# The norms at the entry of the second mixer: tile 0 finished ahead of tile 1's statistics, and a gate tile moved behind tile 1's transposes

## What is computed

```python
h = layer_norm(DEEPNORM_ALPHA * h + squared_relu_mlp(h, ...), ln_mlp_g[1], ln_mlp_b[1])
...
h = rms_norm(x, norm1_w[l]) * (1.0 + sc1) + sh1
...
proj = h @ w_in          # q, k, v of one branch, q, k, v and gate z of the other, more
```

## Time and profile before

| | us |
|---|---|
| median of 3 runs | 1381.76 (1381.08 to 1386.42) |
| the profiled execution's own time | 1387.08 |
| its span | 1385.3 |
| PE busy | 1334.1 (96% of the span) |
| DVE busy | 990.7 (72%) |
| ACT busy | 735.1 (53%) |

### The profile page before, as it was taken

The page is one execution under the profiler, slowest core; times in us unless marked ns, Lnnn a source line. Parts: engine busy times, 40 slices in busy tenths (PEclk is TensorE's granted clock), DMA queues, the critical chain, the costliest instruction groups (busy, mean ns, idle before and its releaser), DMA issues.

```text
span 1385.3 us, 19114 instructions
## 1 busy us (share of the span) xinstructions
PE 1334.1 (96%) x8084; PEld 1168.8 (84%) x8084; DVE 990.7 (72%) x1119; ACT 735.1 (53%) x777; POOL 131.0 (9%) x119
## 2 busy tenths in 40 slices
PE   7999999999999999999999899999999999999996
PEld 7999877799998798799998698788878888878885
DVE  6987564767878735867855745646477788888896
ACT  6655763344444546444444355734434577677673
POOL 0002543110001000100000100015200000000000
PEclk9999999999999999999999989999999999999999
DMA  8552224377877542357775254321254699999993
GB/s 331 183 185 94 95 89 158 146 285 286 310 274 294 192 152 92 122 213 273 277 252 195 103 196 149 106 93 61 66 189 157 217 353 352 335 333 346 345 364 119
DMA packets 41768, 290.29 MB, mean 210 GB/s; under 512 B 4653, under 2 KB 5061, under 8 KB 7632
## 3 DMA queue, kind: packets, MB, share of 16 engines
q1 hardware_dynamic: 35712, 252.76, 49.7%
q0 software_dynamic: 5968, 36.27, 7.0%
HBM read 286.90 MB, written 2.11 MB: 209 GB/s over the span
## 4 chain that ended last, share of the span: by engine, by line
PE 85%; DVE 9%; ACT 3%; DMA 1%; issue 1%; POOL 1%; DVEq 0%; SPq 0%; ACTq 0%; POOLq 0%
PE banks L835 24%; PE banks L837 24%; PE banks L836 24%; DVE w_lo L1617 2%; PE banks L1380 2%; PE banks L1483 1%; DMA raw<-weights 1%; ACT w_hi L392 1%; PE banks L987 1%; DVE mod L1856 1%; DVE pre_norm L1771 1%; PE banks L1163 1%; POOL tiny L2388 1%; PE banks L996 1%; PE banks L890 1%
## 5 line engine op out<-in xcount | busy, mean ns | idle before, releaser
L1617 DVE TENSOR_TENSOR w_lo<-raw,w_hi 128x2048 fp32r<-128x2048 f32 x237 | 542.3, 2295 | 120.6 <-ACT w_hi L392 119.4
L392 ACT ACTIVATE w_hi<-raw 128x2048 fp32r<-128x2048 f32 x237 | 449.9, 1909 | 24.8 <-DMA raw<-weights 24.8
L835 PE MATMUL banks<-hT_hi,w_hi 128*128 128x256 f32 x1120 | 323.8, 289 | 3.3 <-DVE w_lo L1648 3.3
L837 PE MATMUL banks<-hT_hi,w_lo 128*128 128x256 f32 x1120 | 320.0, 286 | 0.0
L836 PE MATMUL banks<-hT_lo,w_hi 128*128 128x256 f32 x1120 | 320.0, 286 | 0.0
L835 PEld LDWEIGHTS banks<-hT_hi,w_hi 128*128 128x128 f32 x1120 | 218.1, 195 | 8.2 <-issue 4.9
L836 PEld LDWEIGHTS banks<-hT_lo,w_hi 128*128 128x128 f32 x1120 | 218.1, 195 | 1.4
L837 PEld LDWEIGHTS banks<-hT_hi,w_lo 128*128 128x128 f32 x1120 | 217.7, 194 | 0.0
L835 PE MATMUL banks<-w_hi,act_hi 128*128 128x512 f32 x256 | 100.2, 391 | 0.4 <-DVE act_lo L1827 0.4
L836 PE MATMUL banks<-w_lo,act_hi 128*128 128x512 f32 x256 | 100.0, 391 | 0.0
L837 PE MATMUL banks<-w_hi,act_lo 128*128 128x512 f32 x256 | 99.7, 389 | 0.0
(11 more groups left out here) (417 smaller groups left out, 2184.2 us busy)
## 6 DMA issues: line engine op xcount, KB each, us to landing
raw<-weights SPq DMA_DIRECT2D x238, 1024.0 KB, 4.8
mod_raw<-weights POOLq DMA_DIRECT2D x24, 1024.0 KB, 5.1
ln_gain_bias<-ln_rows POOLq DMA_DIRECT2D x4, 1024.0 KB, 7.0
h<-x SPq DMA_DIRECT2D x2, 512.0 KB, 4.1
h<-x POOLq DMA_DIRECT2D x1, 1024.0 KB, 5.5
rms_gain<-rms_rows POOLq DMA_DIRECT2D x2, 512.0 KB, 6.2
h_rows<-h POOLq DMA_DIRECT2D x1, 1024.0 KB, 4.4
bias_rows<-bias_table POOLq DMA_DIRECT2D x1, 1024.0 KB, 12.4
```

What stands on the lines that cost most here:

```text
L392: A(hi[u % RING][:, :], raw[u % RING][:, :], ACT.Copy).then_inc(S["w_hi_done"], 1)
L835: mm(out, a[0], b[0], start=start, stop=False)
L837: return mm(out, a[1], b[0], start=False, stop=stop)
L1617: tt(lo[u % RING][:, :], raw[u % RING][:, :], hi[u % RING][:, :].bitcast(F32), ALU.subtract).then_inc(S["w_lo_done"], 1)
```

## The change

On PE, `va_zb_tile(3, 0)` moves ahead of the three tile-1 products, so that it stands directly behind tile 1's transposes. On DVE, `ln_sum` takes a choice of halves; tile 1's first half stays between `rms_mean(0, 0)` and `rms_shift(0, 0)`, its second half moves behind `rms_shift(0, 0)`, and `tile_low(4, 0, 4)` moves ahead of `ln_stats(1)`. Nothing is changed on ACT, POOL and SP, nor in any split.

```diff
             to_T_tile(4, 1, hn0, 16, 4)
+            va_zb_tile(3, 0)
             for n in range(3):
                 va_zb_tile(n, 1).then_inc(S["unit_done"], 1)
-            va_zb_tile(3, 0)
             va_zb_tile(3, 1).then_inc(S["unit_done"], 1)
...
-            def ln_sum(r, t, last_unit, banks):
+            def ln_sum(r, t, last_unit, banks, parts=(0, 1)):
...
-                for c, s in halves():
+                for c, s in halves()[parts[0]:parts[-1] + 1]:
...
             rms_mean(0, 0)
-            ln_sum(3, 1, at("va"), 4)
+            ln_sum(3, 1, at("va"), 4, (0,))
             rms_shift(0, 0)
+            ln_sum(3, 1, at("va"), 4, (1,))
+            tile_low(4, 0, 4)
             ln_stats(1)
-            tile_low(4, 0, 4)
             ln_gain(3, 1)
```

## The result

Over 22 runs each, the changed kernel takes 1390.35 us (1384.24 to 1394.3), the kernel before 1385.97 (1380.8 to 1390.37). The ratio is 1.0037, 95% interval 1.0024 to 1.005: slower by 5.1 us (3.3 to 6.9; the medians differ by 4.4), which is at most the 0.5% from which the forecast called a change clearly slower. The forecast change of +4.23 us lies in that interval. The forecast time of 1386.0 and its range up to 1390 do not hold the measured 1390.35.

A forecast was written before the change was run, and what follows sets the result against it. PE was taken to bound the kernel, holding 85% of the chain. The terms -1.36 + 3.88 + 1.71 = +4.23 us, put on the median 1381.76, gave 1386.0 us, range 1382.5 to 1390.

The forecast's parts named there:

- first product of tile 0: PE behind tile 0's transposes: starts 1.36 us sooner, since DVE makes the first low half before tile 1's statistics.
- what it is worth at the second transposes: Time gained by PE when tile 1's transposes start: -1.36 us, bounds -0.68 and -2.39 depending on the half-clock stretch.
- the wait before zb 1: PE behind tile 1's transposes: the moved product waits for weight unit zb 1's low half, 3.88 us longer than before.
- the clock behind it: PE's products after the new wait: half clock costs 1.71 us, half of 3.42, with bounds 0 and 3.42.
- sum, at the narrow product: All terms together, +4.23 us, bounds +1.49 and +6.62; the trace reads it at the seam's first 8-column product.
- The third hole: PE's 0.98 us wait behind tile 1's transposes for that tile's first low half; forecast to become 4.86 us.
- the 115th low half: DVE's low half of weight unit zb 1, forecast to begin at 793.00 and be ready at 795.29.
- the count of splits: Weight splits DVE had done by 792: units 0 to 114, so the moved product's unit 115 was not ready.
- The cost of the DVE edit for tile 1: Tile 1's later statistics and shift on DVE: hidden under tile 0's 36 products, cost nothing, at most 0.9 us.
- What was released later: ACT's va copies, SP's ka loads and the splits behind them come later; some 10 us of cover, cost nothing.
- The two terms with bounds: The front gain, -1.36 us (-0.68 to -2.39), and the clock loss behind the new wait, +1.71 us (0 to 3.42).
- the reading with the smallest gain: Front of the seam: the half-clock stretch ends at the same moment as before, so 1.36 us are worth 0.68.

The follow-up runs named there:

- The controls: The kernel before and the changed kernel, each unchanged, run again on the chip of the other runs: 1386.96 us and 1389.28 us.
- the repaired versions: Changed kernel, zb 1's split early (0.9994); that plus 12 unread products before tile 0's transposes (0.9992); kernel before, zb 0's tile-0 product behind second transposes (1.001).

## Why the prediction was right and wrong

| step | forecast, us | trace after, us | how read |
|---|---|---|---|
| first product of tile 0 | -1.36 | -1.24 | 8.83 against 10.07 from the modulation sums |
| what it is worth at the second transposes | -1.36 (-0.68 to -2.39) | -0.86 | 19.62 against 20.48 |
| the wait before zb 1 | +3.88 | +3.98 | 5.99 against 2.01 |
| the clock behind it | +1.71 (0 to 3.42) | +2.59 | 16.32 against 13.73 |
| sum, at the narrow product | +4.23 (+1.49 to +6.62) | +5.71 | 41.93 against 36.22 |

**What held.** The third hole became a wait for the 115th low half, of the size that the count of splits and three durations gave, and nothing passed it. The chain has 0.14 us from the end of the low half to PE's product, where I had put 0.05, a hand-over that stood in no row. The cost of the DVE edit for tile 1 was nothing in the changed kernel, though the delay was 0.4 us over the forecast. What was released later cost nothing either: up to 900 us no wait of PE is new but the one for zb 1. The clock did fall. By the Trainium skill ("TensorE: Matmul & The Clock Gate", section "Why this matters for your kernels") idle gaps between bursts of matmuls lower the clock, and the trace agrees: 0.83 behind the hole, 1.00 where it was filled. The two terms with bounds lie inside them, off by 0.5 and 0.9 us. The front is worth less, since products ran at half pace from 778.03 to about 783.3, 14.1 us behind the start of the modulation sums and so nearly as late as before (14.6): close to the reading with the smallest gain, -0.68. Behind the hole they ran at half pace from 794.81 to about 800.1, 5.3 us, where I had taken 3.42.

**What failed.** The step that put the time out of the range is the base: "so I put the same sum on the median", with "a median may be off by a microsecond or two". That median came from three runs, 1381.08, 1381.76 and 1386.42. Over 22 runs it is 1385.97, 4.2 us higher, nearer to the profiled execution (1387.08), which I had taken for the upper end. On that base the sum's own bounds would have been 1387.5 to 1392.6, around the measured 1390.35. The controls show what such runs differ by: stretches outside the seam, 5 us ahead of it and 5 us behind it. The runs that I had showed two levels 5 us apart and I had one trace, of the upper one; a range that took in both would have reached 1393.

Two terms of the sum were mis-sized as well, both to the same side: the gain at the front (-1.36, measured -0.86) and the clock behind the hole (+1.71, measured +2.59). They make the seam's 5.71 out of the forecast 4.23. That 1385.97 + 4.23 = 1390.2 comes so near to the measured 1390.35 is therefore partly luck: the spread outside the seam is larger than what the terms were off by, and the change in time is known only to lie from 3.3 to 6.9 us.

**What stays open.** With the PE edit alone the time is 11 us longer for 6 at the seam. The traces put the rest outside the seam, where executions of the kernel before differ as much; why that kernel has the longer lengths in most of its executions, the runs don't settle. Nor can the runs tell the repaired versions (0.9994, 0.9992, 1.001) from the kernel before; only the traces order them.

## What to carry to other kernels

Before you move a product into a hole, look up when its operands are ready, the weights too: count the preparations on the engine that makes them, and see behind what they are queued. Here the preparation of the moved unit stood behind the very copies whose wait it was to hide. And when runs of one program lie at levels some us apart, the base of a forecast is all of them, not the median of the few.

## What the runs showed of the hardware

A wait of 4.95 us cost 2.4 to 2.6 us more in the 60 products behind it, which ran at 0.50 for 5.3 us, and 20 added products in the hole gave that back at the seam. The clock also fell where PE was busy all the time, within or behind a product of 32 columns at a time, and how long it stayed low differs from execution to execution of one program (3.4 us and 10.0 us at the same place). Because of such stretches, spans say little about a change of this size: the PE edit alone has a span of 1395.9 us and the same kernel with its hole filled 1383.4, 12.5 us less, of which only 2.5 lie in the seam; 5.5 lie ahead of it and 4.5 behind.

POOL's power on a 128 x 1 tile took 0.54 us behind 3.0 to 4.8 us without work on POOL and 1.5 us behind 5.3 us or more, in each of the 14 traces at the seam. That the pause makes the difference is not tested, and spans on POOL are rough; but at tile 1's layer norm DVE waited 0.50 us for the long one and not at all for the short one.
